# Thirteen fixed expert chunks per layer, with six small experts two to a chunk, in a two-block transformer kernel

## The reference, cut to what matters

```python
def hier_moe(h, rg_w, rg_b, re_w, re_b, w_gate, w_up, w_down):   # 512 tokens of width 1024
    ...
    g_p, g_idx = lax.top_k(g_prob, 1)                   # one of 4 groups
    ...
    top_p, top_i = lax.top_k(jax.nn.softmax(e_sel, axis=-1), TOP_K)   # 2 of its 4 experts
    top_p = top_p / jnp.sum(top_p, axis=-1, keepdims=True)
    ...
    def step(acc, xs):                                  # over the 16 experts
        wg, wu, wd, cw = xs                             # 1024x256, 1024x256, 256x1024
        y = (jax.nn.silu(t @ wg) * (t @ wu)) @ wd
        return acc + y.astype(jnp.float32) * cw[:, None], None
```

## Time and profile before

| | |
|---|---|
| median of three runs | 2025.09 us (2023.55 to 2025.58) |
| profiled execution: its span (its own time is not listed) | 2022.0 us |
| median above that span | 3.1 us |
| PE busy | 98% of the span |
| MoE stage, layer 0 | 1378.7 to 1567.2 us in the span (rows of the trace) |
| MoE stage, layer 1 | 1817.7 to 2005.1 us |

### The profile page before, as it was taken

One profiled execution on the slowest core, in us unless ns is written; L12 is line 12 of the kernel. 1 busy time (PEld: TensorE's weight loads), 2 busy tenths in 40 slices (PEclk: granted clock), 3 DMA queues, 4 the chain that ended last, 5 costly groups with the idle time before them and its releaser, 6 DMA issues.

```text
span 2022.0 us, 25679 instructions
## 1 busy us (share of the span) xinstructions
PE 1977.7 (98%) x9120; PEld 1075.8 (53%) x9120; DVE 762.4 (38%) x1660; ACT 561.9 (28%) x1227; POOL 730.7 (36%) x1057
## 2 busy tenths in 40 slices
PE   9999999999999999999999999999999899989998
PEld 6545556655465455566554556545445444445444
DVE  1344433333202344333464638435322411334234
ACT  3234332215112343322152316422111311122110
POOL 1767676757575767676300121001101000001001
PEclk9999999999999999999999999999999999989999
DMA  7332434242355333433754220118996521139995
GB/s 289 113 123 84 161 105 152 89 177 102 133 177 165 142 122 123 141 115 109 276 215 163 78 83 1 64 38 325 386 368 227 222 83 42 63 132 363 368 366 201
DMA packets 74030, 337.95 MB, mean 167 GB/s; under 512 B 8712, under 2 KB 11206, under 8 KB 59334
## 3 DMA queue, kind: packets, MB, share of 16 engines
q1 hardware_dynamic: 41688, 216.98, 28.7%
q0 software_dynamic: 27920, 103.82, 14.6%
q10 hardware_dynamic: 4320, 15.73, 1.9%
HBM read 292.47 MB, written 44.04 MB: 166 GB/s over the span
## 4 chain that ended last, share of the span: by engine, by line
PE 91%; DVE 4%; DMA 2%; issue 2%; ACT 1%; DVEq 1%; PEldq 0%; SPq 0%; PEld 0%; ACTq 0%; POOLq 0%
PE psA L464 25%; PE psA L1730 10%; PE psA L456 9%; PE psA L1860 9%; PE psA L1767 6%; PE psA L627 5%; PE psSO L1875 5%; PE psT L443 3%; PE psA L505 3%; PE psSO L534 3%; PE psSO L544 2%; PE psT L1841 1%; DVE pool_mem L2707 1%; PE psSO L565 1%; PE psSO L600 1%
## 5 line engine op out<-in xcount | busy, mean ns | idle before, releaser
L464 PE MATMUL psA<-gB,pool_mem 128*128 128x512 f32 x1024 | 455.3, 597 | 0.0
L395 POOL TENSOR_TENSOR pool_mem<-pool_mem,cs 128x256 f32<-128x256 f32 x448 | 269.6, 635 | 125.6 <-DMA pool_mem<-in_mod_w 125.0
L464 PEld LDWEIGHTS psA<-gB,pool_mem 128*128 128x128 f32 x1024 | 189.5, 190 | 224.2 <-issue 224.2
L399 POOL TENSOR_TENSOR pool_mem<-pool_mem 128x256 f32<-128x256 f32 x336 | 248.9, 769 | 30.9 <-issue 22.9
L1730 PE MATMUL psA<-pool_mem 128*128 128x512 f32 (+1 forms) x528 | 210.4, 558 | 5.7 <-DVE pool_mem L2305 2.3
L1860 PE MATMUL psA<-pool_mem 128*128 128x512 f32 x448 | 196.9, 592 | 0.0
L456 PE MATMUL psA<-pool_mem,gB 128*128 128x256 f32 (+2 forms) x768 | 189.6, 403 | 1.6 <-ACT gB L797 1.6
L456 PEld LDWEIGHTS psA<-pool_mem,gB 128*128 128x128 f32 x768 | 143.9, 190 | 43.5 <-issue 7.1
L1730 PEld LDWEIGHTS psA<-pool_mem 128*128 128x128 f32 x528 | 100.5, 192 | 109.7 <-issue 99.5
L1681 POOL DMA_INDIRECT pool_mem<-xs_scratch,idx x4 | 3.9, 966 | 364.3 <-DVE idx L2439 363.7
L1860 PEld LDWEIGHTS psA<-pool_mem 128*128 128x128 f32 x448 | 82.9, 190 | 93.7 <-issue 93.7
(11 more groups left out here) (334 smaller groups left out, 2494.6 us busy)
## 6 DMA issues: line engine op xcount, KB each, us to landing
pool_mem<-in_w_gu SPq DMA_DIRECT2D x32, 2048.0 KB, 10.0
pool_mem<-in_mod_w POOLq DMA_DIRECT2D x56, 1024.0 KB, 7.8
pool_mem<-in_w_dn SPq DMA_DIRECT2D x32, 1024.0 KB, 13.6
pool_mem<-in_w_qk SPq DMA_DIRECT2D x24, 1024.0 KB, 4.9
ys_scratch<-pool_mem ACTq DMA_DIRECT2D x30, 512.0 KB, 9.8
ys_scratch<-pool_mem POOLq DMA_DIRECT2D x1, 12288.0 KB, 44.9
pool_mem<-in_odd_w_in SPq DMA_DIRECT2D x5, 2048.0 KB, 13.7
pool_mem<-in_w_out SPq DMA_DIRECT2D x4, 2048.0 KB, 8.4
```

The source lines that it names most:

```text
L395: nc.gpsimd.tensor_tensor(wm[:, b, k], wm[:, b, k], c_all[:, k].to_broadcast([P, MCH]), ALU.mult)
L399: nc.gpsimd.tensor_tensor(wm[:, b, k], wm[:, b, k], wm[:, b, n + k], ALU.add)
L464: m = nc.tensor.matmul(psA[:, n % 2, :], w(i), src[:, k, :], start=(i == 0), stop=(i == len(ks) - 1))
```

## The change

The number of chunks is fixed at 13 per layer, written out in the code of every engine instead of the loop. Experts are ranked: 0 to 3 come first, then those with more than 64 rows, then the others. The first ten ranks get a chunk of 128 rows each (F), the last six share three chunks (P), 64 rows each. The order is in `ORDER`, so the pairs are the fifth, eighth and eleventh chunk (c = 4, 7, 10). Rows that fit neither go to up to nine overflow chunks in a branch after the thirteen; with these inputs there are none, since the first four and the others with more than 64 rows are nine experts in layer 0 and ten in layer 1, and no expert has more than 128 rows.

```diff
+FULL, HALF = 10, 64
+PAIRED = EXPERTS - FULL
+STATIC = 4
+ORDER = "FFFFPFFPFFPFF"
...
-            def load_expert(l, e, b, used=None):
-
-                if used is not None:
-                    sp.wait_ge(yc_half[l][1], used)
...
+            def load_expert(l, u):
+
+                b = u % EXP_BUFS
+                if u >= EXP_BUFS:
+                    sp.wait_ge(yc_half[1], RUNS * l + RUN_OF[USES[u - EXP_BUFS]] + 1)
+                if USES[u] < STATIC:
+                    e = slice(USES[u], USES[u] + 1)
+                else:
+                    e = ds(ranked_expert(sp, USES[u]), 1)
```

On PE a pair's products are done in column halves, each with its own weights:

```diff
                     for k in range(KD):
-                        m = nc.tensor.matmul(psA[:, b, :], xgT[:, b, k, :], gu_w[w][:, k, :],
-                                             start=(k == 0), stop=(k == KD - 1))
-                    m.then_inc(gu_ready[l], 1)
+                        for r, lo, hi in PARTS[c]:
+                            m = nc.tensor.matmul(psA[lo:hi, b, :], xgT[:, b, k, lo:hi], gu_w[USES.index(r) % EXP_BUFS][:, k, :],
+                                                 start=(k == 0), stop=(k == KD - 1))
+                    m.then_inc(gu_ready, 1)
...
-                pe.wait_ge(hot_ready, 2 * l + 1)
-                for s in range(TOP * NT):
-                    m = nc.tensor.matmul(psS[:, 1, 0:CHUNKS - EXPERTS], slot_hot[:, s, :], chunk_hot[:, s, EXPERTS:],
-                                         start=(s == 0), stop=(s == TOP * NT - 1))
-                m.then_inc(idx_ready, 1)
...
+                n = overflow(pe)
+                with pe.Fori(0, 1) as z:
+                    with pe.If(z < n):
...
+                with pe.Fori(0, OVER) as i:
+                    with pe.If(i < n):
```

The removed products at L1886 (7 columns) made the indices of chunks beyond 16; those for overflow chunks are now made in the branch behind the thirteen. DVE has the same two loops there, ACT, POOL and SP one of nine iterations. PE's drain and all of the combination follow these loops. On DVE `places()` is longer and stands elsewhere:

```diff
-                n = chunks(dve)
                 rows_out(0, 0, singly=True)
-                places()
                 rows_out(1, 1)
                 times_up(0, 0)
...
+                places()
                 weights()
                 last_weights()
-                with dve.Fori(0, (CHUNKS + EXP_BUFS) // EXP_BUFS) as i:
...
+                for c in range(RUNS - 2):
+                    rows_out(c + 2, c % 2)
+                    hidden_out(c, c % 2)
+                    times_up(c + 1, 1 - c % 2)
+                    output(c, c % 2)
...
+                n = overflow(dve)
+                with dve.Fori(0, 1) as z:
+                    with dve.If(z < n):
+                        overflow_hot()
+                with dve.Fori(0, OVER) as i:
+                    with dve.If(i < n):
```

More of the change, by code:

```diff
@@ L1348, in second_block @@
+    ahead, beats, beaten = table(NT, EG * EG), table(NT, EG), table(NT, EG)
+    first2, where = table(NT, EG), table(TOP * NT)
+    assert tab_free[0] <= 12296
     slot_hot = part(4096, TOP * NT, P)
@@ L1852, in gate_up_first, with weights, gate_up @@
                     if ks[-1] == KD - 1:
-                        m.then_inc(gu_ready[l], 1)
-                def gate_up(c, b, w, use):
+                        m.then_inc(gu_ready, 1)
+                def weights(c):
+                    for r, _, _ in PARTS[c]:
+                        u = USES.index(r)
+                        pe.wait_ge(exp_loaded[u % EXP_BUFS], LOADED * l + 32 * (u // EXP_BUFS + 1))
+                def gate_up(c):
+                    b = c % 2
                     for half in range(2):
-                        pe.wait_ge(xt_done[l][half], c + 4)
-                    pe.wait_ge(exp_loaded[l][w], 32 * use)
+                        pe.wait_ge(xt_done[half], (RUNS + 3) * l + c + 4)
+                    weights(c)
@@ L1878, in down @@
-                        m.then_inc(yc_half[l][half], 1)
-                turn_rows(0, 0, 1, first=True)
+                            for r, lo, hi in PARTS[c]:
+                                m = nc.tensor.matmul(psO[lo:hi, half, :], hidT[:, b, k * P + lo:k * P + hi],
+                                                     down_w[USES.index(r) % EXP_BUFS][:, k, half * 512:half * 512 + 512],
+                                                     start=(k == 0), stop=(k == 1))
+                        m.then_inc(yc_half[half], 1)
@@ new lines, in last_up @@
+                        for r, lo, hi in PARTS[c]:
+                            m = nc.tensor.matmul(psT[lo:hi, b, 0:D_EXP], xgT[:, b, k, lo:hi], gu_w[USES.index(r) % EXP_BUFS][:, k, D_EXP:],
+                                                 start=(k == 0), stop=(k == KD - 1))
+                    m.then_inc(gu_ready, 1)
+                for c in range(RUNS - 2):
+                    turn_rows(c + 2)
+                    turn_hidden(c, c % 2)
+                    gate_up(c + 1)
+                    down(c)
@@ new lines, in places @@
+                    nc.vector.tensor_tensor(out, low16, along(nch, EXPERTS, EXPERTS), ALU.mult)
+                    dve.drain()
+                    nc.vector.tensor_reduce(incl, out, AX.X, ALU.add)
+                    dve.drain()
+                    out = big[:, 0:OVER * EXPERTS].rearrange("p (m e) -> p m e", m=OVER)
+                    nc.vector.tensor_tensor(out, each(mno, EXPERTS), along(incl, OVER, EXPERTS), ALU.is_ge)
+                    nc.vector.tensor_tensor(excl, incl, nch, ALU.subtract)
@@ L2478, in places @@
                     dve.drain()
[L2480 to L2481 removed]
+                    nc.vector.tensor_scalar(relm[:], slot, float(LAST_END), None, ALU.subtract)
                     dve.drain()
```

540 lines of the change are left out of this document (304 added, 236 removed).

## The result

The changed kernel takes 2053.85 us (median of four runs, 2050.03 to 2055.26) against 2024.69 us before: a ratio of 1.0141, 95% interval 1.0127 to 1.0156. It is slower, as forecast, but by 29 us and not by 13; the forecast was 2038 us with a range up to 2052, so the time lies just outside. The profiled execution has a span of 2052.6 us, 30.6 more than the one of before.

A forecast was written before the change was run, and what follows sets the result against it. PE was taken as the bound, busy 98% of the span, with DMA engines having nothing to spare. Three chunks saved (-34.2) against added waits and costs gave +6.8 us a layer, +13.6 in all: 2038 us, range 2010 to 2052.

The forecast's parts named there:

- (b): Start of the stage on DVE: `places()` and the weights now come before `down(0)`, making it later by 5.6 us a layer.
- (d): Pairs c = 7 and c = 10: two experts' weights needed at once, PE waits 9.7 us each, +19.4 us a layer.
- (e): Single weight loads: less time between release and need, up to about 2 us at three or four places, +3 a layer.
- (f): Pairs' half products on PE: halves overlap at no cost, but changes between full and half cost +2.0 us a layer.
- (g): Tail, ahead of the combination: empty overflow loops delay PE's comb transposes, +6.2 us a layer.
- (c): PE's lower clock after a wait: +1.6 us a layer behind the later `down(0)`, +3.2 behind the two pairs' waits.
- (a): PE's work in the MoE stage: three chunks fewer at 11.4 us each, -34.2 us a layer.
- The rival of faster transfers: Pairs' weights land sooner, waits of 5 us each instead of 9.7, single loads cost nothing: 2014 us; chance 0.20.
- The rival without overlap: Half products don't run side by side, a pair costs a second `gate_up` and `down`: near 2095 us; chance 0.04.
- The rival of a cheap tail: Empty overflow loops cost 1 or 2 us instead of 6.2, start at its lower end: about 2026 us; chance 0.12.
- The rival of late stores: Output stores land late at the pairs, whose waits reach 12 us: about 2050 us; chance 0.12.

The follow-up runs named there:

- The kernel with filled waits: Changed kernel with products that nobody reads put into four of PE's long waits a layer; 2037.05 us, ratio 1.0058 to the kernel before.
- The separate release: Changed kernel with gate and up weights released and awaited apart from the down weights; 1988.8 us, ratio 0.9818 to the kernel before.
- the guard: Changed kernel with the loop of nine overflow iterations inside one more branch on every engine; 2039.5 us, ratio 1.0065 to the kernel before.
- the pairs apart: Changed kernel with only the order changed, pairs in fifth, ninth and thirteenth place; 2025.61 us, ratio 0.9997 to the kernel before.

## Why the prediction was too low

The forecast named the waits that came, and most of their sizes. Against each term, by the same rows, in us a layer:

| step | forecast | layer 0 | layer 1 |
|---|---|---|---|
| (b) later `down(0)` | +5.6 | +4.9 | +4.9 |
| (d) pairs' weights | +19.4 | +20.8 | +21.9 |
| (e) single loads | +3.0 | +4.5 | +4.6 |
| (f) pairs' products, and what is left | +2.0 | +2.6 | +2.6 |
| (g) empty loops | +6.2 | +4.9 | +4.4 |
| (c) clock behind all waits | +4.8 | +8.9 | +15.3 |

(a) is 3 x 11.4 = -34.2 in all columns. For (b) I took the distance from the first transposes of the stage to `down(0)`, 1406.44 - 1381.09 = 25.35 us against 1399.18 - 1378.72 = 20.46; in layer 1 it grew by 7.7 us, of which 2.8 are slow products and stand in (c). For (c) I took the time of a group over that of the same records at the full clock, for instance 8.62 - 7.09 at c = 7. Two smaller things lie outside the table. Layer 0's stage starts 2.4 us late for differences that lie ahead of it. And the part between the two stages became 3.4 us shorter: before, 5.0 us were lost in slow products just ahead of layer 1's stage (1805 to 1817 us), and now 1.7. So of the 15.3 us of layer 1 some 3 are a loss that had been there before and only moved into the stage. The forecast missed the span by 17.0 us and the median by 15: the median lay 3.1 us above the profiled span before and lies 1.3 above it now, so the profiled execution of before had been a fast one, and that hid 2 us.

**The step that failed is (c) with its size and its places.** I priced a wait at 1.6 us, from one wait of 2.61 us, and put that price behind `down(0)` and behind two pairs only. First, the price: after the longer waits the same products lost 2.5 to 3.0 us at `down(0)` and 1.5 to 2.6 us at the pairs. Second, the places: the tail has such a wait too, and there it cost 2.2 and 2.4 us in the combination's first products and another 0.5 in the transposes; in layer 1 a wait of 2.0 us at c = 4 cost 1.7, and 2.8 went at the start (5.62 us for eight records at L1887 against 3.67, and 1.97 against 1.09 for the transposes ahead of them). Over both layers that is 24 us, or 21 without what only moved, instead of 9.6. These 11 us are most of the 17 by which the span missed the forecast; the pairs' and single loads' waits are another 7, the late start of layer 0 2.4 and (f) 1.2, and (b) and (g) gave back 4.5. It is also why PE's busy time fell by 46 us and not by 55 to 65. The kernel with filled waits bears the size out for the places that it fills: 16.8 us of an expected 19.

**(d) was sized well, though not by its bytes.** SP's queue behind the release of the pair c = 7 (L1610 gate and up weights, L1611 down weights; the rows at 1462.27 and 1463.99 are its two experts, the one at 1474.61 is the next):

```profile
1462.27 0.34 SPq L1610 DMA_DIRECT2D pool_mem<-in_w_gu  x1
...
1463.99 0.34 SPq L1610 DMA_DIRECT2D pool_mem<-in_w_gu  x1
...
1474.61 0.34 SPq L1610 DMA_DIRECT2D pool_mem<-in_w_gu  x1
```

From the end of `down(4)` at 1461.5 to the pair's first product at 1486.9 there are 25.4 us, where I had 22.2; for c = 10 it is 22.6 us. The windows of the DMA engines around it (columns as in the earlier trace rows):

```profile
1462.00:1475.00 13.00, 12.38 (x41) 6.14 (x39) 3.98 (x10) 1.89 (x5) 1.15 (x2) 1.00 0.93 362
1475.00:1487.00 12.00, 0.09 (x2) 0.12 (x4) 1.48 (x5) 1.50 (x4) 2.22 (x4) 0.70 1.01 355
1487.00:1500.00 13.00, 13.00 (x50) 5.28 (x51) 1.80 (x3) 0.38 (x1) 0.00 (x0) 0.88 0.48 201
```

They are full, at 362 and 355 GB/s, as long as PE waits, and idle for half of the time behind. The rival of faster transfers would have needed 417 GB/s. The mean from release to need was 352 GB/s at c = 7 and 389 at c = 10, and 374 and 392 in layer 1, so the 394 that I took for the bytes was too high for the first pair's wait and about right for the second. My bytes were too few: in these 25.5 and 22.6 us the engines carried 9.0 and 8.8 MB (352 x 25.5 and 389 x 22.6), where I had 7.3; rows and outputs of two chunks and a part of the next load fall into that time, not 1.0 MB. The forecast did not lean on this sum but on the stretch of 21.8 us in the trace, and so came out near.

The Trainium skill ("DMA: Bandwidth & Descriptors", Specifications) gives roughly 358 GB/s as the limit of a core's HBM. The means at c = 7 look like it, but the trace does not agree: PE's wait at c = 10 in the same stage saw 413 GB/s (1524 to 1533 us) and still lasted 8.8 us. By the page's figure each wait would have been 9.4 us, and the measured ones are 8.8 to 12.2.

But I took the distance of 12.5 us for given, and with it bytes and distance looked like one thing. The separate release shows that they are two: the same transfers, the larger part started an iteration earlier and the smaller wanted an iteration later, cost no wait at all. That also bears on (e): single loads were late by 0.5 to 2 us for the same reason.

**(f) holds.** With no wait ahead of them, half records take 42.5 us / 192 = 221 ns and full ones 112.5 / 256 = 439 ns: two halves side by side cost one full product with 512 moving columns too. In the same kernel the iterations at a pair, from transposes to transposes, take 11.74, 11.63 and 11.46 us against 11.40 for a full one, 0.63 us a pair or 1.9 us a layer, as forecast (+2.0). The rival without overlap is out.

**(g) was somewhat high.** The transposes moved by 4.9 and 4.4 us, since PE's sequencer starts its loops while `down` is still running. The rival of a cheap tail was wrong, as the guard's 14 us show; of these, about 5 are the clock. On DVE the same loops cost more than I had: nine iterations start from 1576.0 to 1584.0, 1.0 us each instead of 0.75, against 0.8 us on PE, and `first_rows` moved by 8.2 us and not by 6.8. No product of PE waited for it.

**The rival of late stores** came near the measured time for another reason. Its waits of 12 us are there at c = 7, but a weight load ends them. DVE does wait for a store ahead of `output` four times in layer 0, 1.2 to 1.9 us, and no row of PE shows a wait for `output`.

**What stays open:** why the pair c = 7 takes 25 us from release to landing and c = 10 only 23, for about the same bytes. The load before it, which ended only at about 1463, is a candidate: the rate from 1462.3 to 1465 was only 140 GB/s. Another is the next load, issued at 1474.61 while the pair's was still under way; no run took them apart.

## What to carry to other kernels

When a change takes work away from the engine that is the bound but leaves the buffers as they are, work out for each load the time between its release and its need in the new order, not only the bytes: here 28 us hung on the places of three pairs in the order, and 65 us on releasing and awaiting the two parts of a buffer separately. Price every new wait of PE with what follows it, up to 3 us of slower products, and look for new waits outside the stage's loop as well, at its start and in its tail. A loop that is passed empty is not free where nothing covers it: test once around it.

## What the runs showed of the hardware that I had not expected

What a wait costs behind it is not a function of its length. A wait of 2.03 us at c = 4 in layer 1 was followed by products of 8.78 us instead of 7.09, and the same wait of 2.03 us in the version with the guard by 7.09; with the pairs apart a wait of 3.37 us cost nothing behind it and one of 2.23 us cost 1.7. After 12 us the loss was 1.5 us in one layer and 2.6 in the other. So a price for it can only be given as a range, nothing to 3 us for waits of 2 us and more. Over the execution the mean granted clock fell from 0.994 to 0.976, and filling four waits a layer with products that nobody reads brought it back to 0.994 and won 17 us. No record is faster for that, only the slow ones are gone.
